# Latent attention's scores as three split fp32r products, with one PSUM copy moved from VectorE to ScalarE and the latents' squares added on GpSimd

## The chip, the cores and the metric

One core of a Trainium2 chip runs the whole program. The metric is the device time of one execution in microseconds (us). The kernel before was executed three times; what counts is the median. A further execution was profiled, and all rows below come from that one.

## The reference, cut to what matters

The program is two transformer blocks on 256 tokens (plus 16 meta tokens in the first), with a model width of 1024: a state-space mixer, an MLP, multi-head latent attention (MLA), an MLP, and then a block with neighbourhood attention, a short gated convolution and an MLP. The change lies nearly all in the latent attention:

```
q_lat, kv_lat, k_pe = split(h @ w_in, [384, 640])
q  = rms_norm(q_lat, q_a_g) @ w_q_b      # 16 heads x 96
kv = rms_norm(kv_lat, kv_a_g) @ w_kv_b   # 16 heads x (64 + 64)
k  = concat(k_nope, k_pe for all heads); v = the other 64
q, k = rms_norm(q, q_norm_g), rms_norm(k, k_norm_g)
q, k = the last 32 of each turned by the rotary angles
p  = softmax(q @ k.T * 96 ** -0.5, causal, two query blocks of 128)
o  = (p @ v) @ w_out
```

## The kernel before, in words

**Split products.** Every weight page (128 partitions x 1024 elements) is loaded by SP into `w_raw`, rounded by ScalarE (ACT) to fp32r (`w_hi`, helper `hi`), and VectorE (DVE) subtracts to get the rest (`w_lo`, helper `lo`). TensorE (PE) then forms hi*hi + hi*lo + lo*hi as three fp32r matmuls. Activations are split the same way. Other matmuls (scores, values, transposes) take plain fp32 operands; such a matmul appears as two records in the trace.

**The attention's steps.** PE, ACT and DVE each run their own hand-written loop over steps t = 0 to 21 (22 on ACT and DVE). GpSimd (POOL) follows them with a short list. Heads come in pairs i = 0 to 7. An even step t = 2i makes keys and values of pair i (`key_unit`), an odd step t = 2i + 1 its queries (`query_unit`). The work of a pair is spread over later steps:

- ACT squares the raw keys or queries (`unit_square`), DVE sums them (`unit_sum`, `k_ss` or `q_ss`), ACT takes logarithm and exponential (`unit_inv`, `k_inv` or `q_inv`), DVE scales in the next step (`unit_scaled`, `k_n` or `q_n`). Rotary turning of the queries is on DVE for the first three pairs (`turn_query`), on POOL afterwards (`query_rope`).
- PE transposes them (`turn_keys` in step 2i + 1, `turn_queries` at the end of step 2i + 2) into one PSUM area, `turned`, that keys and queries share.
- ACT scales that area into SBUF (`unit_final(t - 1)`: `k_fin` in step 2i + 1, `q_fin` in step 2i + 2). In every odd step but one this comes after `unit_inv(t)`, which itself waits for DVE's sum; step 15 has the two the other way round.
- PE makes the scores of head n in step n + 3 (`scores`), DVE masks them and takes the maximum in step n + 4 (`maxima`), ACT exponentiates (`exps`), DVE normalises in step n + 5 (`weigh`), PE transposes the probabilities in step n + 6 (`p_transposes`).
- The transposed probabilities go from PSUM to SBUF in two copies, 128x384 on DVE (`p_t_copy`) and 16x256 on ACT (`p_t0_copy`); PE multiplies them with the values once per pair (`values`), and ACT and DVE split the result (`o_high`, `o_low`).

The output projection (`mout_part`) is cut into parts that run among the last steps.

**Places that the prediction speaks of.** `scores` L740, `turn_keys` L713 with its wait for `qfin_done`, `turn_queries` L731 with its wait for `kfin_done`, PE's loop L804, `unit_final` L1266, `p_t0_copy` L1292, ACT's loop L1302, `unit_sum` L1770, `unit_scaled` L1816, `p_t_copy` L1850, DVE's loop L1860. Before the loop, PE sums squares of the latents over partitions with one-column fp32 matmuls: six matmuls at L658 for keys and values, six at L673 for queries (`q_stat`). At the program's start DVE makes the rest of the first small weight page (`lo(Page(0))`) after the last two `raw_lo`. In the second block's projections DVE makes `yb_lo` at the end of loop turns 11 and 12, and begins each of the turns 8 to 15 with the copy `p_t2` out of PSUM.

## Time and profile before

| | us |
|---|---|
| median of 3 runs | 1103.89 (1103.84 to 1104.99) |
| profiled execution, its own time | 1103.82 |
| span of the profile, first to last instruction | 1102.1 |
| PE busy | 1094.4 (99%) |
| DVE busy | 771.8 (70%) |
| ACT busy | 653.9 (59%) |
| POOL busy | 170.6 (15%) |

The span is 1.7 us shorter than the execution's time. The profile's times for one matmul overlap the next (about 280 ns of duration at about 120 ns from start to start), so costs on PE are read from start to start. A busy time of 99% on PE says that hardly anything else shows as a wait; DVE and ACT have slack on average, and the question is how that slack lies in the attention's steps, at 456 to 545 us of the span.

### The profile page before, as it was taken

The page shows a single profiled execution, that of the slowest core. Times are in us where ns is not written, and L with a number is a line of the kernel's source. Part 1 is how long each engine was busy: PE and PEld are TensorE (multiplying, and loading weights), DVE is VectorE, ACT ScalarE, POOL GpSimd, SP SyncE. Part 2 cuts the span into 40 slices and gives each one's busy share as a digit, 9 for nine tenths or more (in the row PEclk, how much of TensorE's full clock was granted, in tenths as well). Part 3 has the DMA queues.
Part 4 walks back from the last instruction along what each step waited for, and adds up shares of the span by engine and source line. Part 5 has one row for each costly group of instructions (what it writes and reads, how often), then busy time and mean ns, then how long its engine had stood idle before and what let it go on. Part 6 is the DMA issues. An engine that isn't in the chain of part 4 may idle for free.

```text
span 1102.1 us, 24005 instructions
## 1 busy us (share of the span) xinstructions
PE 1094.4 (99%) x8963; PEld 1066.9 (97%) x8963; DVE 771.8 (70%) x1153; ACT 653.9 (59%) x1075; POOL 170.6 (15%) x152
## 2 busy tenths in 40 slices
PE   9999999999999999999999999999999999999998
PEld 8999999999999999988899999999999999999998
DVE  8999999778665555688676665558787687666543
ACT  7899999555554343577565554446555755554331
POOL 0445444326000000111010000000003201000000
PEclk9999999999999999999999999999999999999999
DMA  7454444575454555332265555555444555555552
GB/s 267 181 186 163 169 157 173 153 249 172 171 171 172 179 178 175 136 135 98 83 218 177 189 189 181 180 193 173 153 154 154 185 181 190 180 182 191 187 180 90
DMA packets 53226, 189.96 MB, mean 172 GB/s; under 512 B 5920, under 2 KB 7200, under 8 KB 53168
## 3 DMA queue, kind: packets, MB, share of 16 engines
q1 hardware_dynamic: 51408, 182.59, 48.4%
q0 software_dynamic: 1760, 6.59, 2.1%
q8 instruction: 38, 0.62, 0.2%
q14 instruction: 20, 0.16, 0.0%
HBM read 188.07 MB, written 1.08 MB: 172 GB/s over the span
## 4 chain that ended last, share of the span: by engine, by line
PE 85%; DVE 10%; ACT 2%; issue 2%; DMA 1%; POOL 0%; SPq 0%; DVEq 0%; ACTq 0%
PE lin L462 27%; PE lin L464 26%; PE lin L463 26%; DVE w_lo L1430 3%; DMA w_raw<-w 1%; PE ps L561 1%; DVE s_m L1836 1%; DVE x_lo L1440 1%; DVE p_t L1854 1%; ACT w_hi L948 0%; ACT pr L1351 0%; DVE s_m L1918 0%; PE ps L540 0%; DVE p_t L1941 0%; DVE q_ss L1779 0%
## 5 line engine op out<-in xcount | busy, mean ns | idle before, releaser
L1430 DVE TENSOR_TENSOR w_lo<-w_raw,w_hi 128x1024 fp32r<-128x1024 f32 (+3 forms) x318 | 392.6, 1237 | 237.6 <-ACT w_hi L948 236.6
L948 ACT ACTIVATE w_hi<-w_raw 128x1024 fp32r<-128x1024 f32 (+2 forms) x342 | 352.0, 1034 | 230.9 <-PE lin L464 222.0
L462 PE MATMUL lin<-x_hi,w_hi 128*128 128x256 f32 (+1 forms) x1504 | 432.1, 287 | 0.4 <-DVE x_lo L1440 0.4
L464 PE MATMUL lin<-x_hi,w_lo 128*128 128x256 f32 (+1 forms) x1504 | 428.3, 285 | 0.0
L463 PE MATMUL lin<-x_lo,w_hi 128*128 128x256 f32 (+1 forms) x1504 | 427.3, 284 | 0.0
L462 PEld LDWEIGHTS lin<-x_hi,w_hi 128*128 128x128 f32 x1504 | 283.6, 189 | 2.2 <-issue 0.8
L464 PEld LDWEIGHTS lin<-x_hi,w_lo 128*128 128x128 f32 x1504 | 283.8, 189 | 0.0
L463 PEld LDWEIGHTS lin<-x_lo,w_hi 128*128 128x128 f32 x1504 | 283.0, 188 | 0.6
L464 PE MATMUL lin<-hid_hi,w_lo 128*128 128x256 f32 (+1 forms) x768 | 218.2, 284 | 0.0
L463 PE MATMUL lin<-hid_lo,w_hi 128*128 128x256 f32 (+1 forms) x768 | 217.9, 284 | 0.0
L462 PE MATMUL lin<-hid_hi,w_hi 128*128 128x256 f32 (+1 forms) x768 | 217.4, 283 | 0.0
L464 PEld LDWEIGHTS lin<-hid_hi,w_lo 128*128 128x128 f32 x768 | 145.1, 189 | 0.0
L462 PEld LDWEIGHTS lin<-hid_hi,w_hi 128*128 128x128 f32 x768 | 145.0, 189 | 0.0
L463 PEld LDWEIGHTS lin<-hid_lo,w_hi 128*128 128x128 f32 x768 | 144.3, 188 | 0.0
L2060 POOL TENSOR_TENSOR h_sq<-h_sq 128x256 f32<-128x256 f32 (+1 forms) x35 | 30.7, 878 | 448.1 <-ACT h_sq L961 446.6
L1171 ACT ACTIVATE relu<-lin 128x512 f32<-128x512 f32 (+1 forms) x48 | 29.1, 606 | 82.6 <-PE lin L464 82.6
L2065 POOL TENSOR_TENSOR w_lo<-w_raw,w_hi 128x1024 fp32r<-128x1024 f32 x24 | 58.4, 2437 | 70.2 <-ACT w_hi L948 70.0
L957 ACT ACTIVATE x_hi<-h,vecs 128x256 fp32r<-128x256 f32 (+2 forms) x40 | 20.3, 507 | 41.6 <-DVE h L1708 37.7
L462 PE MATMUL lin<-g_hi,w_hi 128*128 128x272 f32 x144 | 42.3, 294 | 0.1
L1691 DVE TENSOR_TENSOR hid_lo<-relu_sq,hid_hi 128x512 f32 (+1 forms) x48 | 34.4, 717 | 11.2 <-DVE relu_sq L1687 11.2
L464 PE MATMUL lin<-g_hi,w_lo 128*128 128x272 f32 x144 | 41.7, 289 | 0.0
L463 PE MATMUL lin<-g_lo,w_hi 128*128 128x272 f32 x144 | 41.4, 288 | 0.0
(301 smaller groups left out, 1505.5 us busy)
## 6 DMA issues: line engine op xcount, KB each, us to landing
w_raw<-w SPq DMA_DIRECT2D x342, 512.0 KB, 3.3
acs_bc<-acs_dram POOLq DMA_DIRECT2D x8, 544.0 KB, 5.9
bias_mask<-rpb POOLq DMA_DIRECT2D x4, 512.0 KB, 10.9
h<-h SPq DMA_DIRECT2D x4, 272.0 KB, 3.7
out<-h SPq DMA_DIRECT2D x8, 128.0 KB, 3.3
cst<-const SPq DMA_DIRECT2D x1, 808.0 KB, 7.1
vecs<-vec SPq DMA_DIRECT2D x1, 131.5 KB, 2.1
w_raw<-w SPq DMA_DIRECT2D x1, 128.0 KB, 4.7
```

Of the source, the lines that this page charges most:

```text
L462: mm3(o, wh, xh, start=first and i == 0, stop=False)
L463: mm3(o, wh, xl, start=False, stop=False)
L464: ins = mm3(o, wl, xh, start=False, stop=last and i == kts - 1)
L561: nc.tensor.matmul(o[rows, 0:T], x_tok[:, 0, j * HD:(j + 1) * HD], mm[:, j, 0:T], start=True, stop=False)
L948: a(w_hi[pg.slot][:, 0:n], w_raw[pg.slot][:, 0:n], ACT.Copy).then_inc(w_hi_done, pages)
L957: a(x_hi[:, kt.value, 0:width(norm)], h[:, kt.value, tokens(norm)], ACT.Copy, scale=gain(norm, kt.value)).then_inc(xh_done, 1)
L1171: a(relu[i][:, :, 0:n], linp(k, slice(0, n)), ACT.Relu).then_inc(drained[k.parity], 1)
L1430: tt(w_lo[pg.slot][:, 0:n], w_raw[pg.slot][:, 0:n], w_hi[pg.slot][:, 0:n].bitcast(F32), ALU.subtract)\
L1440: stt(x_lo[:, kt.value, 0:n], h[:, kt.value, tk], gain(norm, kt.value), x_hi[:, kt.value, 0:n].bitcast(F32), ALU.mult, ALU.subtract).then_ ...
L1691: tt(hid_lo[:, bass.ds(at.value, 2), 0:n], relu_sq[i][:, :, 0:n], hid_hi[:, bass.ds(at.value, 2), 0:n].bitcast(F32), ALU.subtract).then_in ...
L2060: tt(h_sq[:, 0, 0:n], h_sq[:, 0, 0:n], h_sq[:, kt, 0:n], ALU.add).then_inc(hsum_done, 1)
L2065: tt(w_lo[pg.slot][:, 0:n], w_raw[pg.slot][:, 0:n], w_hi[pg.slot][:, 0:n].bitcast(F32), ALU.subtract)\
```

## The change

Scores: queries and keys are kept as fp32r pairs (`q_hi`, `q_lo`, `k_hi`, `k_lo`) and each of a head's two products becomes three. ACT's `unit_final` writes the rounded part; a new `unit_low` on DVE subtracts it from the same PSUM area, and only DVE's write now sets `kfin_done` and `qfin_done`. The 128x384 copy of the probabilities goes to ACT, ahead of the 16x256 copy. POOL adds neighbouring squares of latents, so that PE sums three columns in place of six at the first place and four in place of six at the second. Parts of the output projection, the split of the first page and `yb_lo` are put elsewhere in their engines' order.

```diff
-        q_fin = [sb(f"q_fin{i}", [QK, 4, T2], F32, mla) for i in range(2)]
-        k_fin = [sb(f"k_fin{i}", [QK, 4, T], F32, mla) for i in range(2)]
+        q_hi = [sb(f"q_hi{i}", [QK, 4, T2], F32R, mla) for i in range(2)]
+        q_lo = [sb(f"q_lo{i}", [QK, 4, T2], F32R, mla) for i in range(2)]
+        k_hi = [sb(f"k_hi{i}", [QK, 4, T], F32R, mla) for i in range(2)]
+        k_lo = [sb(f"k_lo{i}", [QK, 4, T], F32R, mla) for i in range(2)]
...
-            pe.wait_ge(latsq_done, 1)
+            pe.wait_ge(latsum_done, 1)
             for b, t0 in enumerate(MLA_BLOCKS):
-                for i in range(2):
-                    ins = nc.tensor.matmul(ps5[:, b:b + 1], lat_sq[:, i, t0:t0 + P], ones[:, 0:1],
-                                           start=i == 0, stop=i == 1)
+                ins = nc.tensor.matmul(ps5[:, b:b + 1], lat_sq[:, 0, t0:t0 + P], ones[:, 0:1], start=True, stop=True)
...
-                pe.wait_ge(latsq_done, 3)
+                pe.wait_ge(latsum_done, 2)
...
-                    for i in range(3):
+                    for i in range(2):
...
-                nc.tensor.matmul(o[:, 0:144], q_fin[p][:, j, 0:128], k_fin[p][:, j, 0:144], start=True, stop=True)
-                nc.tensor.matmul(o[:, 144:416], q_fin[p][:, j, 128:256], k_fin[p][:, j, :],
-                                 start=True, stop=True).then_inc(s_done, 1)
+                for to, queries, keys in ((slice(0, 144), slice(0, 128), slice(0, 144)),
+                                          (slice(144, 416), slice(128, 256), slice(0, T))):
+                    for i, (q_, k_) in enumerate(((q_hi, k_hi), (q_hi, k_lo), (q_lo, k_hi))):
+                        ins = mm3(o[:, to], q_[p][:, j, queries], k_[p][:, j, keys], start=i == 0, stop=i == 2)
+                ins.then_inc(s_done, 1)
...
-                if t == 17:
-                    mout_part(0, 5, 0)
...
                 if 3 <= t < 19:
                     scores(t - 3)
+                if t == 16:
+                    mout_part(0, 4, 0)
...
-                    mout_part(0, 2, 5)
+                    mout_part(0, 3, 4)
...
-                    a(q_fin[s % 2][:, hs, :], turned, ACT.Copy, scale=v(V_QG, rows=slice(0, QK))).then_inc(qfin_done, 1)
+                    a(q_hi[s % 2][:, hs, :], turned, ACT.Copy, scale=v(V_QG, rows=slice(0, QK))).then_inc(qhi_done, 1)
...
+                a(p_t[n % 2][:, :], ps7[:, 0:384], ACT.Copy).then_inc(pt_done, 1)
                 a(p_t0[n % 2][0:META, :], ps4[0:META, 256:512], ACT.Copy).then_inc(pt0_done, 1)
...
+            lo(Page(0), DT_PAGE)
+            dve.sem_inc(w_lo_done[1], 1)
             raw_lo(6)
             raw_lo(7)
-            lo(Page(0), DT_PAGE)
-            dve.sem_inc(w_lo_done[1], 1)
...
+            def unit_low(un):
+
+                i, s = un // 2, un // 4
+                j0 = 2 * (i % 2)
+                hs = slice(j0, j0 + 2)
+                if s >= 2:
+                    dve.wait_ge(s_done, 4 * (s - 2) + j0 + 2)
+                if un % 2:
+                    dve.wait_ge(qhi_done, i + 1)
+                    stt(q_lo[s % 2][:, hs, :], turned, v(V_QG, rows=slice(0, QK)),
+                        q_hi[s % 2][:, hs, :].bitcast(F32), ALU.mult, ALU.subtract).then_inc(qfin_done, 1)
+                else:
+                    dve.wait_ge(khi_done, i + 1)
+                    stt(k_lo[s % 2][:, hs, META:T], turned, v(V_KG, rows=slice(0, QK)),
+                        k_hi[s % 2][:, hs, META:T].bitcast(F32), ALU.mult, ALU.subtract)
+                    stt(k_lo[s % 2][:, hs, 0:META], turned_meta, v(V_KG, rows=slice(0, QK)),
+                        k_hi[s % 2][:, hs, 0:META].bitcast(F32), ALU.mult, ALU.subtract).then_inc(kfin_done, 1)
...
-                if t == 15:
-                    p_t_copy(t - 6)
...
-                if 6 <= t < 15 and t % 2:
-                    p_t_copy(t - 6)
...
-                if 6 <= t < 16 and not t % 2 or 16 <= t < MLA_STEPS:
-                    p_t_copy(t - 6)
+                if 1 <= t <= 16:
+                    unit_low(t - 1)
...
+            add_latents(0, 1)
             pool.wait_ge(kpe_step, 2)
...
+            add_latents(4, 3)
             pool.wait_ge(kpefin_done, 3)
```

`yb_lo` moves from the end of turns 11 and 12 to turns 12 and 13, right after the copy `p_t2`. `add_latents(to, count)` waits for `count` of the squares and adds two 128x272 tiles on POOL.

DVE's order at the end of an odd step, here t = 7 (sum of the queries' squares) and the start of the next. Before:

```order
L1430 TENSOR_TENSOR w_lo<-w_raw,w_hi 128x576 [waits w_hi_done]
L1854 COPY p_t<-ps 128x384 [waits pT_done]
L1779 TENSOR_REDUCE q_ss<-q_sq 128x4 [waits qln_done,qsq_done]
L1823 TENSOR_TENSOR q_n<-lin,q_inv 128x384 [waits qT_done,qinv_done]
L1858 TENSOR_TENSOR o_lo<-ps,o_hi 128x256 [waits oh_done]
```

With the change:

```order
L1435 TENSOR_TENSOR w_lo<-w_raw,w_hi 128x576 [waits w_hi_done]
L1784 TENSOR_REDUCE q_ss<-q_sq 128x4 [waits qln_done,qsq_done]
L1868 SCALAR_TENSOR_TENSOR k_lo<-lin,vecs,k_hi 96x2x256 [waits khi_done]
L1870 SCALAR_TENSOR_TENSOR k_lo<-ps,vecs,k_hi 96x2x16
L1828 TENSOR_TENSOR q_n<-lin,q_inv 128x384 [waits qT_done,qinv_done]
L1875 TENSOR_TENSOR o_lo<-ps,o_hi 128x256 [waits oh_done]
```

The copy has left, and between the sum and the scaling of the queries stand two subtractions that wait for ACT's `k_hi`.

ACT's order in the same odd step, with the change (squares of the queries to the rounding of the keys):

```order
L1245 ACTIVATE q_sq<-lin 128x4x96 [waits qss_done,w_used]
L1300 ACTIVATE p_t<-ps 128x384 [waits pT_done]
L1301 ACTIVATE p_t<-ps 16x256
L1292 ACTIVATE pr,rsum<-s_m,nmx 128x144 [waits pT_done,sm_done]
L1292 ACTIVATE pr,rsum<-s_m,nmx 128x272
L1256 ACTIVATE q_ln<-q_ss 128x4 [waits qss_done]
L1260 ACTIVATE q_inv<-q_ln,eps_t 128x4 [waits qn_done,qln_done]
L1282 ACTIVATE k_hi<-lin,vecs 96x2x256 [waits kT_done]
L1283 ACTIVATE k_hi<-ps,vecs 96x2x16
```

The order is that of before but for the 128x384 copy, which is new here; `k_hi` has the place that `k_fin` had, behind `q_ln` and `q_inv`.

DVE's order at the end of an even step (sum of the keys' squares), before, in t = 6:

```order
L1787 TENSOR_REDUCE k_ss<-k_sq 128x6 [waits kln_done,ksq_done]
L1798 TENSOR_TENSOR v_tok<-lin,kv_inv 128x384 [waits w_used]
L1854 COPY p_t<-ps 128x384 [waits pT_done]
L1830 TENSOR_TENSOR k_n<-lin,k_inv 128x6x64 [waits kT_done,kinv_done]
```

With the change:

```order
L1792 TENSOR_REDUCE k_ss<-k_sq 128x6 [waits kln_done,ksq_done]
L1803 TENSOR_TENSOR v_tok<-lin,kv_inv 128x384 [waits w_used]
L1864 SCALAR_TENSOR_TENSOR q_lo<-lin,vecs,q_hi 96x512 [waits qhi_done]
L1835 TENSOR_TENSOR k_n<-lin,k_inv 128x6x64 [waits kT_done,kinv_done]
```

`q_lo` takes the place of the copy, with a wait for ACT's `q_hi`.

## Rows read from the trace of the kernel before

**Rows 1.** The page: the granted clock of TensorE over 40 slices, in tenths.
```profile
PEclk9999999999999999999999999999999999999999
```

**Rows 2.** Timeline of PE, steps 12 and 13: start us, duration us, line, tiles, records.
```profile
503.93 0.39 PE L682 MATMUL lin<-w_hi,l_hi 128*128 128x256 f32 x1
...
506.15 0.41 PE L754 MATMUL ps<-k_fin,q_fin 96*128 96x144 f32 x2
...
506.86 0.27 PE L768 MATMUL ps<-cst,pr 128*16 128x128 f32 x1
...
513.24 0.38 PE L682 MATMUL lin<-w_hi,l_hi 128*128 128x256 f32 x1
```

**Rows 3.** Timeline of DVE, end of step 12 to the start of step 14.
```profile
507.15 0.55 DVE L1787 TENSOR_REDUCE k_ss<-k_sq 128x6 f32<-128x390 f32 x1
...
508.09 0.54 DVE L1854 COPY p_t<-ps 128x384 f32<-128x384 f32 x1
508.55 0.54 DVE L1830 TENSOR_TENSOR k_n<-lin,k_inv 128x384 f32<-128x384 f32 x1
...
511.41 0.55 DVE L1779 TENSOR_REDUCE q_ss<-q_sq 128x4 f32<-128x388 f32 x1
512.56 0.56 DVE L1823 TENSOR_TENSOR q_n<-lin,q_inv 128x384 f32<-128x384 f32 x1 [0.60 <-ACT q_inv L1256]
```

**Rows 4.** Timeline of ACT, the same steps.
```profile
508.11 0.68 ACT L1275 ACTIVATE q_fin<-lin,vecs 96x512 f32<-96x512 f32 x1
...
511.99 0.21 ACT L1252 ACTIVATE q_ln<-q_ss 128x4 f32<-128x4 f32 x1
...
513.00 0.27 ACT L1279 ACTIVATE k_fin<-ps,vecs 96x32 f32<-96x32 f32 x1
```

**Rows 5.** Timeline of DVE: first and last of eight key scalings, last query scaling.
```profile
460.39 0.56 DVE L1830 TENSOR_TENSOR k_n<-lin,k_inv 128x384 f32<-128x384 f32 x1 [0.43 <-ACT k_inv L1264]
...
518.65 0.55 DVE L1830 TENSOR_TENSOR k_n<-lin,k_inv 128x384 f32<-128x384 f32 x1
...
523.13 0.56 DVE L1823 TENSOR_TENSOR q_n<-lin,q_inv 128x384 f32<-128x384 f32 x1 [0.60 <-ACT q_inv L1256]
```

**Rows 6.** DVE's waits, 458 to 522 us: total us, times, longest.
```profile
DVE o_lo L1858 <- ACT o_hi L1300: 4.3, 4, 1.4
...
DVE w_lo L1430 <- ACT w_hi L948: 0.6, 1, 0.6
```

**Rows 7.** Timeline of DVE in the second block: two three-operand instructions in a row.
```profile
756.88 0.88 DVE L1983 SCALAR_TENSOR_TENSOR qk_f<-qk_r,vecs,qk_inv 128x256 f32<-128x256 f32 x2
```

**Rows 8.** Timeline of PE, steps 16 and 17: waits, last query transposes, values.
```profile
524.17 0.27 PE L768 MATMUL ps<-cst,pr 128*16 128x128 f32 x1 [0.39 <-DVE o_lo L1858]
...
525.37 0.64 PE L737 MATMUL lin<-cst,q_n 128*96 128x128 f32 x4 [0.50 <-POOL q_n L2160]
...
529.07 0.65 PE L784 MATMUL ps<-p_t,v_tok 128*64 128x256 f32 x4
```

**Rows 9.** Timeline of DVE and of ACT, steps 16 and 17.
```profile
525.86 1.21 DVE L1430 TENSOR_TENSOR w_lo<-w_raw,w_hi 128x1024 fp32r<-128x1024 f32 x1
526.99 0.29 DVE L1836 CUSTOM_DVE_ANT_0 s_m<-ps,cst 128x144 f32<-128x144 f32 x1
...
527.58 0.15 DVE L1844 RECIPROCAL rinv<-rsum 128x2 f32<-128x2 f32 x1
...
527.69 0.41 ACT L1288 ACTIVATE pr<-s_m,nmx 128x144 f32<-128x144 f32 x1
...
528.61 0.36 ACT L1296 ACTIVATE p_t<-ps 16x256 f32<-16x256 f32 x1
```

**Rows 10.** Timeline of PE at the three smaller places.
```profile
10.40 0.31 PE L505 MATMUL lin<-g_hi,w_hi 128*32 128x272 f32 x1 [0.33 <-DVE w_lo L1430]
...
448.18 1.39 PE L658 MATMUL ps<-cst,h_sq 128*128 128x1 f32 x12
...
833.79 1.08 PE L902 MATMUL ps<-p_t,v 128*64 128x256 f32 x8 [0.66 <-DVE p_t L1941]
```

More of the change, by code:

```diff
@@ L1274, in unit_final @@
                     act.wait_ge(qT_done, i + 1)
-                    a(q_fin[s % 2][:, hs, :], turned, ACT.Copy, scale=v(V_QG, rows=slice(0, QK))).then_inc(qfin_done, 1)
+                    a(q_hi[s % 2][:, hs, :], turned, ACT.Copy, scale=v(V_QG, rows=slice(0, QK))).then_inc(qhi_done, 1)
                 else:
                     act.wait_ge(kT_done, i + 1)
-                    a(k_fin[s % 2][:, hs, META:T], turned, ACT.Copy, scale=v(V_KG, rows=slice(0, QK)))
-                    a(k_fin[s % 2][:, hs, 0:META], turned_meta, ACT.Copy, scale=v(V_KG, rows=slice(0, QK)))\
-                        .then_inc(kfin_done, 1)
+                    a(k_hi[s % 2][:, hs, META:T], turned, ACT.Copy, scale=v(V_KG, rows=slice(0, QK)))
+                    a(k_hi[s % 2][:, hs, 0:META], turned_meta, ACT.Copy, scale=v(V_KG, rows=slice(0, QK)))\
+                        .then_inc(khi_done, 1)
             def exps(n):
@@ L1941, in _ @@
                     nc.vector.tensor_copy(p_t2[i % 2][:, :], ps7[:, :]).then_inc(pt2_done, 1)
+                if i in (12, 13):
+                    j = i - 12
+                    dve.wait_ge(ybh_done, j + 1)
+                    tt(yb_lo[:, 2 * j:2 * j + 2, :], yb[:, 2 * j:2 * j + 2, :],
+                       yb_hi[:, 2 * j:2 * j + 2, :].bitcast(F32), ALU.subtract).then_inc(ybl_done, 1)
                 if i in (11, 12):
@@ L2132, in _, with add_latents @@
                     .then_inc(rope_done, 1)
+            def add_latents(to, count):
+                pool.wait_ge(latsq_done, count)
+                tt(lat_sq[:, to, :], lat_sq[:, to, :], lat_sq[:, to + 1, :], ALU.add).then_inc(latsum_done, 1)
+            add_latents(0, 1)
             pool.wait_ge(kpe_step, 2)
```

17 lines of the change are left out of this document (4 added, 13 removed).

## The prediction, made before the change ran

> **What bounds the kernel now.** I read the page first: TensorE is busy 99% of the span, and its granted clock is full in every slice [rows 1]. Then I read PE's timeline through the attention. Steps 12 and 13 make one pair of heads and take 513.24 - 503.93 = 9.31 us [rows 2], with every product starting right behind the one before: there PE sets the pace. Next come the timelines of DVE and ACT over the same pair, because the change hangs new work on both. They show an order of hand-overs that is nearly as long as PE's work. From one `k_n` to the next there are DVE's instructions, 0.60 us of idleness before `q_n` [rows 3], and a wait of up to 1.4 us for `o_hi` before `o_lo`, four times and 4.3 us in all [rows 6]. The first is a hand-over to ACT and back and cannot shrink. The second is the only slack in the loop; from 508.55 us DVE runs without a gap to the end of `q_ss`. So DVE has about 1 us per pair to give before it sets the pace in place of PE. The question is how much the change puts on it, as work and as waiting.
>
> **Scores on PE.** In step 12 the two fp32 products of a head take 506.86 - 506.15 = 0.71 us from their start to the next work [rows 2]. Afterwards there are six fp32r products at 0.11 to 0.12 us each, 0.69 us. That is 0.02 us a head in the even steps; in odd steps the product's entry behind a transpose of 16 rows is slower now, and 0.2 us could come back. Over 16 heads that is 0.3 to 1.9 us of PE work saved, but worth nothing where PE is made to wait.
>
> **DVE in the odd steps.** Before, `q_ss` starts at 511.41 and `q_n` at 512.56: 1.15 us [rows 3]. In the new order `k_lo` stands between the two and waits for ACT's `k_hi`, which ACT makes only after `q_ln` and `q_inv`, and these wait for `q_ss`. So DVE waits for an ACT chain that it has just set going. From the start of `q_ss` to `q_ln` it is 511.99 - 511.41 = 0.58 us; from there to the end of the last `k_fin`, 513.00 + 0.27 = 513.27, it is 1.28 us [rows 4]; a hand-over costs 0.03 us (`q_inv` to `q_n`). Then the two subtractions. No row shows this form with 512 elements out of PSUM. Two of 256 elements end 0.88 us after the first starts [rows 7], which fits 0.40 us from start to start, or 0.13 us plus 1.04 ns an element: 0.66 us for 512, 0.17 us for 32, both estimates. The bounds are 0.60 (a two-operand instruction's pace) and 0.88 us. Together 0.58 + 1.28 + 0.03 + 0.83 = 2.72 us in place of 1.15: **+1.57 us** in each of the seven odd steps 1 to 13, so +11.0 us. The removed copy, 508.55 - 508.09 = 0.46 us [rows 3], gives back 4 x 0.46 = 1.8 us (steps 7, 9, 11, 13).
>
> The Trainium skill, in "VectorE: DVE Perf Modes", section "The DRAIN you can't avoid", says that a next instruction does not start until the pipe has emptied, save one that is not held. The rows here show starts 0.08 us before the predecessor's end; by the page's rule taken strictly each new subtraction would cost its full duration, about 0.25 us more a pair, and the sum would come out 2 us higher.
>
> **DVE in the even steps.** Before, `k_ss` at 507.15 and the next `k_n` at 508.55: 1.40 us, with the copy in it [rows 3]. Now `q_lo` waits for `q_hi`, whose forerunner ends at 508.11 + 0.68 = 508.79 [rows 4]: 1.64 + 0.03 + 0.66 = 2.33 us, **+0.93 us** in steps 6, 8, 10, 12, 14, and +1.39 us in steps 2 and 4, which had no copy: +7.4 us.
>
> **The loop as a whole.** From the first `k_n` at 460.39 to the eighth at 518.65 it is 58.3 us [rows 5]. Added to DVE's chain are 11.0 - 1.8 + 7.4 = 16.6 us; the waits for `o_hi` (4.3 us) and one for `w_hi` (0.6 us) vanish [rows 6], because those partners are then early. Net **+11.7 us**: 70.0 us for seven pairs. A late pair takes 10.1 us against PE's 9.3, so PE now waits in each, before `turn_keys` (for `q_lo`) or `turn_queries` (for the `q_n` that stands behind `k_lo`). ACT gains two copies of 0.5 us a pair, ahead of waits that it has anyway; their cover is the gap between `q_sq` and `q_ln`. If it is gone, each costs up to 0.5 us, some 2 us in all.
>
> **The end of the loop.** In step 15 ACT makes `k_hi` before `q_inv`; from `k_n` to `q_n`, 4.48 us before [rows 5], goes to about 4.2: -0.3 us. The first part of the projection, 12 products and 1.4 us, now stands in step 16, where PE waits 0.39 and 0.50 us [rows 8]. It covers these waits, but it also stands behind the last `k_lo` and ahead of the last `turn_queries`, which comes about 0.4 us later after `q_n`. From `turn_queries` to `values(5)` it was 529.07 - 525.37 = 3.70 us [rows 8]. The new chain is 0.1, ACT's two copies 0.75, `q_hi` 0.68, `q_lo` 0.69, then on DVE a full `w_lo` 1.13 and `maxima` 0.59, ACT's `exps` 0.92 and only behind them the two copies again, 0.75: 5.7 us [rows 9]. That is +2.0, with the above **+2.4 us**. Lower bound 0 (if later slack takes it), upper 3.5. Three products moved behind the last values add 0.36 and take away a wait of 0.2: +0.2.
>
> **The small parts.** First page earlier: PE waits 0.33 us for it [rows 10]; -0.3 us, nothing behind is late for want of the two `raw_lo`. Squares: the first place loses 6 of 12 records in 1.39 us, -0.65 us; POOL is free from 446 us and its sum, 0.8 us, ends before PE asks at 448.2. The second place saves 0.4 us on PE, but `k_n` does not depend on it: 0. If POOL were late, PE would wait at most 1 us at either. `yb_lo` behind `p_t2` brings that copy 0.6 us forward, against a wait of 0.66 us on PE [rows 10]: -0.6 us, as nothing late waits for `yb_lo` itself.
>
> **Sum:** 11.7 - 0.3 + 2.4 + 0.2 - 0.3 - 0.65 - 0.6 = +12.4 us. On the profiled execution's 1103.8 us, which is the median within 0.1 us, that is **1116.2 us**.
>
> **Rivals.**
> 1. *PE keeps the pace, the change is faster.* This is so if DVE's new waits lie beside its slack. It needs an added chain of under 1 us a pair, where I count over 2; it decides at the `q_ss`, `k_hi`, `k_lo`, `q_n` sequence. For it speaks PE's 99% and DVE's 70%. Then the gains are 0.3 + 0.65 + 0.4 + 0.6 + 0.9 in step 16, and 0.3 to 1.9 for the scores: about -4, **1100 us**. Chance 0.09.
> 2. *Only the first pairs stretch.* They have less PE work, and DVE already sets their pace: three pairs cost 3 x 1.57 + 2 x 1.39 + 0.93 - 0.6 = +7.8 us; the later four (chain +2.0 each, slack 1.1) may be absorbed if the hand-overs are shorter than mine. With the small gains and without the end's term +6: **1110 us**. Chance 0.15.
> 3. *The clock falls.* PE would stand idle for 1 to 2 us in each pair. The rows show the full 2.4 GHz with idle pieces of 0.5 us only [rows 1, 8]. If half the loop ran at 1.2 GHz, some 35 us of PE work would take as long again: **1150 us**. The Trainium skill ("TensorE: Matmul & The Clock Gate", "HAM oscillation") describes a kernel whose waits between groups of matmuls brought the clock down each time. Chance 0.04.
> 4. *The change gives no more than noise*, its terms cancelling: chance 0.02.
>
> My forecast has 0.70; within it the bounds (0.60 to 0.88 us for a subtraction, 0 to 3.5 at the end, up to 2 for ACT) give 1112 to 1120. The range is 1107 to 1120: it takes in rival 2 and leaves out 1 and 3. A measurement here tells 0.2%, 2.2 us, from no change. Faster 0.09, same 0.03, slower 0.88.
>
> **What would show it.** In the profile after: `k_n` to `k_n` near 10 us in late pairs; DVE idle before `k_lo` about 1.3 us, released by ACT `k_hi`, and about 0.7 us before `q_lo`, released by `q_hi`; no more waits before `o_lo` in the loop; PE idle before the transposes, released by `q_lo` and by POOL's or DVE's `q_n`. I am wrong if pairs stay at 9.3 us with PE gapless, if the DVE subtractions take under 0.5 us, or if the span grows outside 440 to 560 us.

## The result, and the profile after

| | before | after |
|---|---|---|
| median, us | 1104.15 (1103.84 to 1104.99) | 1123.08 (1120.64 to 1124.25) |
| ratio | | 1.0168, 95% interval 1.0156 to 1.0181 |
| profiled execution, its own time | 1103.82 | 1122.26 |
| span | 1102.1 | 1120.6 |

Each median is of four executions. The change made the kernel slower by 1.7%. The direction was forecast, the size was not: 1116.2 us were forecast, with a range that ended at 1120.

The span falls into four stretches by three marks on DVE: the first `k_n`, the eighth `k_n` and the last `o_lo` (the start of each). Every profile below is read by them.

| us | to the first `k_n` | seven pairs | close (to the last `o_lo`) | rest |
|---|---|---|---|---|
| before | 460.4 | 58.3 | 25.2 | 558.3 |
| forecast | 459.4 | 70.0 | 27.5 | 557.7 |
| after | 460.0 | 70.6 | 32.0 | 558.0 |

So the loop came out as forecast within 0.6 us, and 4.5 of the profiled execution's 6.1 us above the forecast lie in the close. The page of after, against [rows 1]:

```profile
span 1120.6 us, 24067 instructions
...
PE 1102.3 (98%) x8985; PEld 1074.6 (96%) x8985; DVE 776.8 (69%) x1161; ACT 659.7 (59%) x1091; POOL 172.1 (15%) x154
...
PEclk9999999999999999989899999999999999999999
```

Two slices no longer have the full clock. DVE's timeline answers to [rows 3, 5]: one even step, one odd step, and the first and last `k_n`.

```profile
460.00 0.56 DVE L1835 TENSOR_TENSOR k_n<-lin,k_inv 128x384 f32<-128x384 f32 x1 [0.43 <-ACT k_inv L1268]
...
506.85 0.55 DVE L1792 TENSOR_REDUCE k_ss<-k_sq 128x6 f32<-128x390 f32 x1
508.55 0.75 DVE L1864 SCALAR_TENSOR_TENSOR q_lo<-lin,vecs,q_hi 96x512 fp32r<-96x512 f32 x1 [0.69 <-ACT q_hi L1279]
509.22 0.54 DVE L1835 TENSOR_TENSOR k_n<-lin,k_inv 128x384 f32<-128x384 f32 x1
...
511.60 0.55 DVE L1784 TENSOR_REDUCE q_ss<-q_sq 128x4 f32<-128x388 f32 x1
513.57 0.75 DVE L1868 SCALAR_TENSOR_TENSOR k_lo<-lin,vecs,k_hi 96x512 fp32r<-96x512 f32 x1 [1.42 <-ACT k_hi L1283]
514.24 0.24 DVE L1870 SCALAR_TENSOR_TENSOR k_lo<-ps,vecs,k_hi 96x32 fp32r<-96x32 f32 x1
514.40 0.54 DVE L1828 TENSOR_TENSOR q_n<-lin,q_inv 128x384 f32<-128x384 f32 x1
...
530.57 0.54 DVE L1835 TENSOR_TENSOR k_n<-lin,k_inv 128x384 f32<-128x384 f32 x1
```

From `q_ss` to `q_n` it is 2.80 us (forecast 2.72), from `k_ss` to `k_n` 2.37 (forecast 2.33). A subtraction of 512 elements takes 0.67 us from start to start (forecast 0.66). The next instruction again starts 0.08 us ahead of the recorded end, so the stricter reading of the Trainium skill ("VectorE: DVE Perf Modes", "The DRAIN you can't avoid") does not hold here either. The table of waits, 458 to 562 us (total, times, longest), against [rows 6]:

```profile
DVE k_lo L1868 <- ACT k_hi L1283: 9.8, 8, 1.4
DVE o_lo L1875 <- ACT o_hi L1305: 7.4, 3, 3.4
DVE q_lo L1864 <- ACT q_hi L1279: 7.2, 8, 2.4
PEld lin L728 <- DVE k_n L1835: 6.1, 6, 2.1
...
PE ps L788 <- ACT p_t L1300: 2.4, 1, 2.4
...
PE ps L772 <- ACT p_t L1301: 1.9, 5, 0.7
```

DVE stands still 17 us for the high halves. The last two lines are waits of PE that the forecast does not name: PE waits for ACT's copies of the probabilities. PE's timeline at the close, against [rows 8]:

```profile
533.73 1.12 PE L788 MATMUL ps<-p_t,v_tok 128*64 128x256 f32 x4
...
539.05 0.60 PE L739 MATMUL lin<-cst,q_n 128*96 128x128 f32 x4
540.14 0.27 PE L772 MATMUL ps<-cst,h_sq 128*16 128x128 f32 x1 [0.49 <-ACT p_t L1301]
544.91 1.12 PE L788 MATMUL ps<-p_t,v_tok 128*64 128x256 f32 x4 [2.45 <-ACT p_t L1300]
```

The last queries' transposes (L739) start 8.48 us after the eighth `k_n`, where it was 6.72, and `values(5)` 5.86 us after them, where it was 3.70. The four products of L788 take 1.12 us twice, 0.65 in [rows 8]. The windows of after (length; busy us of PE, PE's weight loads, DVE, ACT and POOL; granted clock, share of DMA, GB/s) show one candidate for the reason:

```profile
462.00:482.00 20.00, 15.29 (x114) 13.94 (x113) 14.46 (x40) 12.28 (x35) 1.02 (x2) 0.91 0.36 121
482.00:500.00 18.00, 17.26 (x134) 15.72 (x133) 14.74 (x49) 12.11 (x39) 2.50 (x6) 0.91 0.29 101
500.00:520.00 20.00, 18.95 (x159) 16.71 (x160) 15.63 (x45) 14.40 (x48) 3.98 (x10) 1.00 0.32 102
520.00:540.00 20.00, 17.80 (x135) 14.50 (x132) 14.78 (x46) 14.68 (x45) 3.45 (x9) 0.91 0.25 84
540.00:560.00 20.00, 16.37 (x116) 14.16 (x117) 8.28 (x29) 8.80 (x26) 0.00 (x0) 0.83 0.17 54
```

With only the levels 2.4 and 1.2 GHz, a mean of 0.91 over 20 us is 3.6 us at the lower one; the four windows below 1.00 make 3.6 + 3.2 + 3.6 + 6.8 = 17 us. The trace places them: the granted clock is 0.50 from 478.5 to 485.3 us in the pairs, and from 533.1 to 536.5 and from 543.4 to 550.2 us in the close. The profiled execution is no exception: over whole executions the mean granted clock was 0.992 to 0.995 in all four of the changed kernel and 0.999 or 1.000 in those of the kernel before. In DVE's timeline of the close the order costs time as well:

```profile
540.66 0.75 DVE L1864 SCALAR_TENSOR_TENSOR q_lo<-lin,vecs,q_hi 96x512 fp32r<-96x512 f32 x1 [2.35 <-ACT q_hi L1279]
541.33 1.21 DVE L1435 TENSOR_TENSOR w_lo<-w_raw,w_hi 128x1024 fp32r<-128x1024 f32 x1
542.46 0.30 DVE L1841 CUSTOM_DVE_ANT_0 s_m<-ps,cst 128x144 f32<-128x144 f32 x1
```

The maxima of head 13, whose scores PE had made by 537.1, wait behind `q_lo` and a weight page. Last, the scores themselves, one head in an even step: 505.15 to 505.86, 0.71 us as in [rows 2]. Six fp32r products take as long as two fp32 products, so PE gains nothing.

```profile
505.15 0.23 PE L759 MATMUL ps<-k_hi,q_hi 96*128 96x144 f32 x1
...
505.86 0.27 PE L772 MATMUL ps<-cst,pr 128*16 128x128 f32 x1
```

### The profile page after: what moved, and what is told of

Same layout as the page of the kernel before. It is cut to its first block, busy times and chain, and to the rows that moved or that the text cites. A ratio compares the mean times of both kernels' runs of the same rounds, so it can differ in the third digit from the quotient of the medians.

```text
span 1120.6 us, 24067 instructions
## 1 busy us (share of the span) xinstructions
PE 1102.3 (98%) x8985; PEld 1074.6 (96%) x8985; DVE 776.8 (69%) x1161; ACT 659.7 (59%) x1091; POOL 172.1 (15%) x154
## 4 chain that ended last, share of the span: by engine, by line
PE 85%; DVE 7%; ACT 2%; issue 2%; DMA 1%; POOL 0%; DVEq 0%; ACTq 0%; SPq 0%
PE lin L466 26%; PE lin L468 26%; PE lin L467 26%; DVE w_lo L1435 2%; DMA w_raw<-w 1%; PE ps L565 1%; DVE s_m L1841 1%; DVE x_lo L1445 1%; ACT q_hi L1279 0%; PE ps L759 0%; PE ps L895 0%; DVE k_n L1835 0%; PE ps L906 0%; PE ps L544 0%; PE ps L881 0%
## 5 line engine op out<-in xcount | busy, mean ns | idle before, releaser
L1696 DVE TENSOR_TENSOR hid_lo<-relu_sq,hid_hi 128x512 f32 (+1 forms) x48 | 34.4, 717 | 11.2 <-DVE relu_sq L1692 11.2
```

The source lines that it names most:

```text
L1696: tt(hid_lo[:, bass.ds(at.value, 2), 0:n], relu_sq[i][:, :, 0:n], hid_hi[:, bass.ds(at.value, 2), 0:n].bitcast(F32), ALU.subtract).then_in ...
```

## The experiments

The four stretches of each profile, the median of the timed executions, and its ratio to the kernel before (1103.9 to 1104.5 us in these runs). The median and the profile are in general different executions. Of hi_first one execution of four took 5774 us, for which nothing on record gives a reason; its median is that of the other three.

| run | first `k_n` | pairs | close | rest | median | ratio (95%) |
|---|---|---|---|---|---|---|
| late_low | 459.9 | 61.6 | 29.4 | 558.1 | 1113.1 | 1.0078 (1.0064 to 1.0092) |
| hi_first | 459.4 | 64.8 | 30.0 | 558.1 | 1117.9 | 1.0124 (1.0106 to 1.0143) |
| late_hi | 460.1 | 63.1 | 29.5 | 558.0 | 1114.1 | 1.0096 (1.0083 to 1.0110) |
| copy_dve | 460.6 | 72.4 | 29.6 | 558.0 | 1123.9 | 1.0184 (1.0170 to 1.0198) |
| late_copy_dve | 461.7 | 64.2 | 31.7 | 558.0 | 1117.2 | 1.0106 (1.0088 to 1.0124) |
| copy_act | 460.7 | 58.2 | 26.4 | 558.3 | 1105.3 | 1.0008 (0.9999 to 1.0017) |
| more_products | 461.9 | 71.1 | 30.0 | 558.0 | 1121.4 | 1.0146 (1.0130 to 1.0161) |
| mout_back | 459.6 | 70.0 | 27.3 | 558.0 | 1119.9 | 1.0151 (1.0132 to 1.0170) |
| close_order | 462.7 | 70.6 | 26.7 | 558.1 | 1119.3 | 1.0135 (1.0115 to 1.0155) |
| late_best | 462.1 | 61.6 | 27.3 | 558.1 | 1110.6 | 1.0051 (1.0036 to 1.0067) |
| small_parts | 459.4 | 58.1 | 25.9 | 558.1 | 1104.7 | 1.0006 (0.9997 to 1.0015) |
| small_lat_yb | 459.6 | 58.1 | 25.2 | 558.1 | 1102.9 | 0.9991 (0.9982 to 1.0000) |
| first_page | 463.1 | 58.3 | 25.2 | 558.4 | 1105.9 | 1.0009 (1.0000 to 1.0018) |
| page_back | 459.4 | 70.1 | 30.9 | 558.0 | 1120.0 | 1.0145 (1.0129 to 1.0160) |

### The loop: order or amount of work

**late_low**, DVE's loop:

```diff
                 if 1 <= t <= 16:
                     unit_scaled(t - 1)
+                if 2 <= t <= 17:
+                    unit_low(t - 2)
...
-                if 1 <= t <= 16:
-                    unit_low(t - 1)
```

> The changed kernel, but DVE writes the low half of a unit's keys or queries one step later, right behind the scaling of the next unit, instead of last in its own step, where it waits for ACT's high half (waits of 1.2 us in the mean for k_hi, 0.9 for q_hi, and all of them stand in the chain). Theory A, the order: the 10.1 to 10.4 us of a pair come from DVE standing still for ACT's high half while the next unit waits behind it. Then a pair falls by about 1.2 us in the odd steps and the whole loop by 6 to 9 us: 1114 to 1117 us, between the two kernels, with the waits of k_lo and q_lo on ACT gone from the table of waits. Theory B, the amount of work on DVE and ACT sets the pair (each low half costs DVE 0.7 to 0.9 us that the kernel before did not have): the waits move to another place and the time stays at 1121 to 1125 us. Against A from the other side: the transposes of the next keys need the low half of the queries read out of the shared bank first, so the low half stands ahead of the transposes now, and 0.6 us of the gain can be lost there.

The order decides: 10 us less in the median with the same instructions, a little more than theory A said. The profile is 11.5 us shorter, 8.9 of them in the pairs. Nothing stands between sum and scaling any more, 1.07 and 1.20 us, and `q_lo` comes with no wait behind `k_n` (DVE's timeline):

```profile
510.30 0.55 DVE L1792 TENSOR_REDUCE k_ss<-k_sq 128x6 f32<-128x390 f32 x1
...
511.37 0.56 DVE L1835 TENSOR_TENSOR k_n<-lin,k_inv 128x384 f32<-128x384 f32 x1
512.02 0.75 DVE L1864 SCALAR_TENSOR_TENSOR q_lo<-lin,vecs,q_hi 96x512 fp32r<-96x512 f32 x1
...
514.61 0.55 DVE L1784 TENSOR_REDUCE q_ss<-q_sq 128x4 f32<-128x388 f32 x1
515.81 0.56 DVE L1828 TENSOR_TENSOR q_n<-lin,q_inv 128x384 f32<-128x384 f32 x1 [0.66 <-ACT q_inv L1260]
```

The granted clock was 1.00 in every window of this profile. The close, 29.4 us, is therefore not to be set against the 32.0 us of after as they stand: further down, 3.5 of those turn out to be the clock, so in the close the later low halves cost about 0.9 us (the last queries' transposes start 9.4 us after the eighth `k_n`, where at full clock it is 7.3). What is left in the pairs, 3.4 us above before, is what the order does not remove. 2.8 of it lie in the first three pairs (6.6, 7.5 and 9.5 us against 5.9, 6.6 and 8.2), the ones of which rival 2 says that DVE sets their pace; that it is DVE's amount of work was argued, not tested.

**hi_first**, ACT's loop: `unit_final(t - 1)` ahead of `unit_inv(t)` in every odd step, not in step 15 alone.

```diff
-                if t == 15:
+                if 1 <= t < 16 and t % 2:
                     unit_final(t - 1)
                 if t < 16:
                     unit_inv(t)
```

> The changed kernel, but in the odd steps ACT writes the keys' high half before the logarithm and the exponential of the queries' norm, instead of behind them. Theory A, the hand-over between ACT and DVE (q_ss, then k_hi, then k_lo, then q_n, 2.72 us where the kernel before took 1.15) sets the odd step: k_lo then runs while ACT makes the queries' norm, and 0.6 to 0.8 us of each odd step goes away, 4 to 5.5 us in all, 1117.5 to 1119 us. Theory B, the amount of work: nothing is removed, so 1122 to 1124 us. A third outcome, the high half comes before the transposes are there and ACT stands still with the norm behind it: a slower kernel, 1124 us or more.

As theory A expected, 1117.9 us. From `q_ss` to `q_n` it is 1.95 us here, 0.85 less than in after; over the seven odd steps it is 6.2 us less, against 5.8 us which the pairs lost. The profiled execution, 1113.9 us, is the fastest of the three by 4 us. DVE's timeline:

```profile
516.28 0.55 DVE L1784 TENSOR_REDUCE q_ss<-q_sq 128x4 f32<-128x388 f32 x1
517.40 0.75 DVE L1868 SCALAR_TENSOR_TENSOR k_lo<-lin,vecs,k_hi 96x512 fp32r<-96x512 f32 x1 [0.57 <-ACT k_hi L1283]
...
518.23 0.55 DVE L1828 TENSOR_TENSOR q_n<-lin,q_inv 128x384 f32<-128x384 f32 x1
```

**late_hi** has both edits, the two diffs above together.

> Both orders together: DVE's low halves one step later, and ACT's high half of the keys ahead of the queries' norm in the odd steps. Alone they gave 10 us and 5 us. If both remove the same wait (DVE's low half of the keys standing still for ACT's high half, 9.8 us in eight waits), the second adds nothing, or costs up to 5 us, since the queries' scaling now waits 0.7 us longer for the norm in every odd step: 1113 to 1118 us. If they remove different waits, the sum shows: 1108 to 1110 us.

The second edit adds nothing to the first and costs 1.5 us in the pairs: both remove the same wait, and `q_n` now waits 8.3 us for `q_inv`, where it was 5.1 in late_low.

### The copy of the probabilities

**copy_act** is the kernel before with the copy on ACT:

```diff
             def p_t0_copy(n):
...
+                a(p_t[n % 2][:, :], ps7[:, 0:384], ACT.Copy).then_inc(pt_done, 1)
...
-                if 6 <= t < 15 and t % 2:
-                    p_t_copy(t - 6)
```

(and so for the other two calls of `p_t_copy` in DVE's loop). **copy_dve** is the changed kernel with the same lines the other way round.

> The changed kernel with the probabilities' 128x384 copy back on DVE in the places of the kernel before, everything else as changed. By the prediction's term the copy is worth 1.8 us on DVE, so this is slower than the changed kernel by about that: 1125 us. Rival, from the trace of the changed kernel: with both copies on ACT the transposes of the next head wait for them (1.9 us in five waits) and the values too (2.4 us in one), mostly behind the last pair, and the close of the stage took 32.0 us from the last scaled keys to the last low half of the outputs, where it was 25.1 us before; with the copy on DVE that close shrinks by 2 to 4 us and the loop grows by up to 2 us, 1120 to 1123 us.

> The kernel before with one part of the change alone: the probabilities' 128x384 copy on ACT. Prediction's term: 1.8 us less on DVE in the pairs' even steps, 1102.4 us. Rival: DVE's place in the pair's chain was hidden or ACT is as full as DVE, 1104 us. Second rival: the close of the stage waits for ACT, which makes each copy behind a weight page's high half or two exponentials, +1 to +4 us, 1105 to 1108 us.

In the changed kernel the pairs grow by 1.8 us with the copy back on DVE, the prediction's term to the tenth, and the close shrinks by 2.4; the medians cannot tell the two kernels apart. Most of the 2.4 us is not the copy: the close of after has 10.2 us at a granted clock of 0.50, that of copy_dve 3.4 us. hi_first, whose instructions in the close stand in the order of after and which also has 3.4 us at 0.50 there, closes in 30.0 us, so about 0.4 us are left for the copy. In the kernel before, the copy on ACT changes nothing in the pairs (58.2 and 58.3 us) and loses 1.3 us at the close: 0.7 ahead of the last queries' transposes, 0.4 from there to `values(5)`, where PE waits for it, and 0.2 behind (PE's timeline of copy_act; no wait before `values(5)` in [rows 8]):

```profile
526.35 0.64 PE L737 MATMUL lin<-cst,q_n 128*96 128x128 f32 x4 [0.50 <-POOL q_n L2149]
530.42 0.65 PE L784 MATMUL ps<-p_t,v_tok 128*64 128x256 f32 x4 [0.41 <-ACT p_t L1296]
```

**late_copy_dve** is late_low with the lines of copy_dve.

> The kernel with the low halves one step later (1113.1 us), and the probabilities' copy back on DVE. In that kernel DVE is the fuller engine of the loop (15.9 to 17.8 us of 20), so by its load 8 copies of about 0.4 us in the even steps cost up to 3 us in the loop. At the close the values wait 1.3 us and the outputs' high half for ACT's copies. If the close decides, 1110 to 1112 us; if the loop decides, 1114 to 1116 us.

The pairs grow by 2.6 us, as DVE's load said. The close did not shrink but grew by 2.2, which neither case foresaw. The growth lies in the two stretches in which the clock was down, from the eighth `k_n` to the last queries' transposes (9.4 to 10.4 us) and from `values(5)` to `values(7)` (13.5 to 14.8 us); between them it is 4.7 us in both. The windows, where late_low had 1.00:

```profile
520.00:540.00 20.00, 16.18 (x122) 13.99 (x118) 16.19 (x48) 12.72 (x34) 3.48 (x9) 0.91 0.25 79
540.00:560.00 20.00, 18.71 (x145) 16.03 (x144) 9.28 (x30) 6.67 (x23) 0.00 (x0) 0.91 0.15 50
```

### The close, and the clock

**more_products** (the diff shows the first of its three places) repeats a unit's first product five times ahead of `query_unit(i >= 1)` and `key_unit(1 to 3)`, one product of `scores(14)` eight times and the last transpose of `p_transposes(11)` eleven times; the results of the repeats are overwritten.

```diff
+                    for _ in range(again if i == 0 else 0):
+                        mm3(o, lh, wh, start=True, stop=True)
                     mm3(o, lh, wh, start=i == 0, stop=False)
```

> The changed kernel with products repeated on TensorE (their first result thrown away) in the places of the loop where PE stood still before the granted clock fell: ahead of the queries' products of each pair, of the keys' products of pairs 1 to 3, of the scores of head 14 and of the last transposes of head 11. It only adds work to PE. Theory C, the granted clock: the changed kernel lost some 3 to 4 us against the forecast to three stretches at 1.2 GHz (17 us in all, of which PE works the smaller part on the path), so with the clock kept at 2.4 GHz it takes 1118 to 1121 us although it does more. Theory D, the excess comes from waits alone: the added products cost 0 to 5 us, 1123 to 1128 us, whatever the clock does. If the clock falls all the same, the run tells nothing between the two.

With more work on PE the median is 1.7 us below the changed kernel's, and the clock stayed at 1.00 up to 540 us (0.91 after it). The time lies between the two cases, nearer to C. The single executions say more: in three of the four the granted clock was 1.00 over the whole execution, and they took 1118.6, 1121.0 and 1121.7 us, where after took 1120.6 to 1124.3 at 0.992 to 0.995. The fourth, the profiled one with 1122.7 us, also has the long `sg` that is described under the small parts. So work added in the places where PE had stood still kept the clock up: PE's standing still is what brings it down here. What that costs, the next two runs show.

**mout_back**, PE's loop:

```diff
+                if t == 17:
+                    mout_part(0, 5, 0)
...
-                if t == 16:
-                    mout_part(0, 4, 0)
...
-                    mout_part(0, 3, 4)
+                    mout_part(0, 2, 5)
```

> The changed kernel with the output's products in the order of the kernel before: none ahead of the last queries' transposes, 15 behind them, 6 instead of 9 ahead of the last values. The prediction took this part of the change at +0.2 us. The kernel with the small parts alone closes the stage 0.8 us later than the kernel before, although its loop is the same. Theory A: the 12 products (1.4 us) stand ahead of the last queries' transposes and hold the whole close up by about 1 us, and the 3 products ahead of the last values by 0.35 us, so undoing them gives 1.0 to 1.4 us: 1121.8 us. Theory B: in the changed kernel PE stands still there for other engines anyway, so the time stays at 1123 us within 0.4, or grows, because the products that filled PE are gone and the granted clock falls more.

**close_order**, DVE's loop: `maxima(13)` and `weigh(12)` ahead of the last `q_lo`.

```diff
-                if 1 <= t <= 16:
+                if 1 <= t < 16:
                     unit_low(t - 1)
-                if t in (16, 17):
-                    lo(At(C_HEAD).page(nxt))
+                if t == 17:
+                    unit_low(15)
+                    lo(At(C_HEAD).page(18))
+                    lo(At(C_HEAD).page(19))
```

> The changed kernel with one step of DVE in another order: the maxima and the weighing of the scores' heads 13 and 12 come ahead of the last low half of the queries, which waited 2.35 us for ACT's high half with them behind it, and the two weight pages' low halves follow it. Theory A, a wait that holds the engine's queue: this gives 1.5 to 2.5 us at the close of the stage (32.0 us from the last scaled keys to the last low half of the outputs in the changed kernel), 1120.5 to 1121.5 us. Theory B, the granted clock made the close long: the close stays at 31 to 32 us and the clock falls in it as before, 1122.5 to 1124 us.

Both medians gained more than either case said, 3.2 and 3.8 us. In close_order PE has the same instructions in the same order as in after, and its windows have the full clock at the close (windows, then PE's timeline):

```profile
520.00:540.00 20.00, 17.62 (x147) 15.13 (x145) 16.90 (x50) 15.81 (x46) 4.00 (x10) 1.00 0.33 106
540.00:560.00 20.00, 17.77 (x149) 15.27 (x148) 8.36 (x30) 10.07 (x31) 0.00 (x0) 1.00 0.15 54
```

```profile
536.26 0.65 PE L788 MATMUL ps<-p_t,v_tok 128*64 128x256 f32 x4
...
540.65 0.60 PE L739 MATMUL lin<-cst,q_n 128*96 128x128 f32 x4
...
544.75 0.65 PE L788 MATMUL ps<-p_t,v_tok 128*64 128x256 f32 x4 [0.68 <-ACT p_t L1300]
...
558.25 0.65 PE L788 MATMUL ps<-p_t,v_tok 128*64 128x256 f32 x4
```

So the two profiles price the clock. From the eighth `k_n` to L739: 540.65 - 533.34 = 7.3 us, 8.5 in after. From `values(5)` to `values(7)`: 558.25 - 544.75 = 13.5 us, 15.9 in after (544.91 to 560.78). Together 3.5 us of after's close are TensorE at 1.2 GHz. Between the two, from L739 to `values(5)`, 4.1 us stand against 5.9: that is the order on DVE, 1.8 us. Page_back (below), in which PE, DVE and ACT have after's order in the close, tells the two apart, because its clock was down in one of the stretches only (windows of page_back):

```profile
520.00:540.00 20.00, 17.22 (x142) 14.61 (x140) 15.45 (x42) 15.11 (x43) 3.50 (x9) 1.00 0.25 80
540.00:560.00 20.00, 17.16 (x125) 14.56 (x125) 6.71 (x28) 7.30 (x25) 0.00 (x0) 0.83 0.16 53
```

The close in five profiles, us, with the mean granted clock of each stretch:

| profile | eighth `k_n` to L739 | L739 to `values(5)` | `values(5)` to `values(7)` |
|---|---|---|---|
| after | 8.5 (0.80) | 5.9 (0.87) | 15.9 (0.83) |
| page_back | 7.3 (1.00) | 5.9 (0.87) | 15.9 (0.83) |
| close_order | 7.3 (1.00) | 4.1 (1.00) | 13.5 (1.00) |
| mout_back | 6.6 (1.00) | 5.8 (1.00) | 13.1 (1.00) |
| before (L737) | 6.7 (1.00) | 3.7 (1.00) | 13.0 (1.00) |

The same instructions in the same order take 1.2 us longer in the first stretch when the clock is down for 3.4 us of it. Mout_back had the full clock from 500 us on as well, and its close, 27.3 us, is 1.2 below the 32.0 - 3.5 = 28.5 of after without its slow stretches: that is the 12 products ahead of the last queries' transposes (0.7) and the three ahead of the last values (0.4). In the pairs the clock cost less: with 6.8 us at 1.2 GHz after and close_order took 70.6 us, with 3.4 us page_back and mout_back took 70.1 and 70.0, and the whole difference is in the third pair (11.2 and 11.3 against 10.7 us).

The clock fell in different places from one execution to the next, also of one kernel. Its mean was 0.997, 0.993, 0.997 and 0.997 in close_order, and in mout_back the time followed it: 1116.7 and 1119.4 us at 0.998, 1119.9 and 1121.3 at 0.995, 1124.0 at 0.992. The profile of mout_back is the fastest of its five executions, so its parts price the edits and its total does not stand for the median.

**late_best** joins late_low, mout_back, and the last `q_lo` behind the weighing (the lines of close_order; the diff is against late_low):

```diff
-                if 2 <= t <= 17:
+                if 2 <= t < 17:
                     unit_low(t - 2)
```

> Low halves one step later on DVE (1113.1 us, close 29.4 us), with the output's products in the order of the kernel before and the last low half of the queries behind the maxima and the weighing. If the waits found in the close are what is left of it: close 26 to 27.5 us, the whole 1110 to 1111.5 us. The loop keeps its 61.7 us against 58.3 us of the kernel before, which is DVE's added work of 0.75 us in every odd step, so no order of this form gets to the kernel before; a time under 1106 us would speak against that.

As expected in the close and in the median, and the granted clock was 1.00 in all five executions. It is the best form of the split that was tried, and still 0.5% behind the kernel before.

### The small parts

**small_parts** is the kernel before with every small part of the change; **small_lat_yb** has the latents' squares and `yb_lo` alone.

```diff
+            def add_latents(to, count):
+                pool.wait_ge(latsq_done, count)
+                tt(lat_sq[:, to, :], lat_sq[:, to, :], lat_sq[:, to + 1, :], ALU.add).then_inc(latsum_done, 1)
```

> The kernel before, with all the small parts of the change and without the split of the scores and without the probabilities' copy on ACT: latents' squares added on GpSimd, the first page's halves in another order, the low half of the inner products moved, the three products of the output moved. By the sum of the prediction: -0.65 (squares), -0.6 (low half of the inner products), -0.3 (first page), +0.2 (three products), so 1.3 us under the kernel before, a ratio of 0.9988. By the trace of the changed kernel, where the first page's 0.39 us are given back by two waits of 0.2 us before 441 us: 1.0 to 1.1 us under, a ratio of 0.9990. If the small parts disturb one another, 0 or slower.

> The kernel before with two of the small parts alone, the latents' squares added on GpSimd (0.65 us by the prediction) and the low half of the inner products moved (0.6 us); the order of the output's products and the first page are those of the kernel before. If the two keep what the trace shows of them, 1.25 us under the kernel before, 1102.9 us, ratio 0.9989, and the kernel beats both. The kernel with all the small parts was level with the kernel before (1.0006), where its moved output products gave back 0.8 us at the close and its first page at most 0.4; so 0.5 us under is the least that this explains. If it is level as well, the gains of these parts are taken by something that no part of the trace names, the arrival of the weight pages first.

Level with all four, 1.1 us gained with two, as expected; with an interval that ends at 1.0000 the gain is at the edge of what can be told here. The output's products give 0.8 us back at the close. By the profile the two parts of small_lat_yb gained unequally. The first `k_n` comes 0.75 us earlier, with the six records at L658 in 0.72 us in place of 1.39. But `yb_lo` gained 0.3 us and not 0.6: the third set of value products at L902 starts 0.6 us earlier after the last `o_lo`, as forecast, the fourth only 0.3, and so it is in every profile with this edit (the rest is 558.0 to 558.1 us against 558.3). What is missing between small_parts and small_lat_yb beyond the 0.8 us was put down to the first page, and tested.

**first_page** is the kernel before with that edit alone, **page_back** the changed kernel without it.

```diff
-            raw_lo(6)
-            raw_lo(7)
             lo(Page(0), DT_PAGE)
             dve.sem_inc(w_lo_done[1], 1)
+            raw_lo(6)
+            raw_lo(7)
```

> The kernel before with one edit: the low half of the first page ahead of the last two residual low halves on DVE. Prediction: -0.3 us, 1103.9 us. Theory E: the edit shifts DVE against GpSimd by a few tenths of a microsecond, and in some executions one DVE instruction near 32 us is then held 2.5 us beside a GpSimd subtraction, which costs some 2 us on PE. Then the single times fall into two groups 2 to 2.5 us apart, a spread that the kernel before does not have (1103.4 to 1105.1 in nearly all executions), and the median is 0.3 to 1.5 us above the kernel before. If the spread stays within 1.5 us and the median within 0.3 us of the kernel before, the first page is not the cause.

> The changed kernel with the first page in the order of the kernel before. Theory E: its 1123.1 us fall by 0.5 to 1.5 us, 1121.6 to 1122.6 us, and the first scaled keys start within 0.5 us of 460 us in the profile. Theory F, the spread comes from the split of the scores and the close alone (the granted clock falls in other places from execution to execution): 1123 us with the same spread of 3.6 us.

The single times of first_page fall into two groups, five at 1103.9 to 1104.8 and six at 1105.9 to 1107.2, as theory E said; the ratio, 1.0009, has an interval that begins at 1.0000. The profiled execution is of the second. Timelines of DVE, POOL and PE in it:

```profile
32.45 3.59 DVE L1543 TENSOR_SCALAR sg<-cv 128x544 f32<-128x544 f32 x2
36.59 1.21 DVE L1430 TENSOR_TENSOR w_lo<-w_raw,w_hi 128x1024 fp32r<-128x1024 f32 x1
...
33.29 2.43 POOL L2065 TENSOR_TENSOR w_lo<-w_raw,w_hi 128x1024 fp32r<-128x1024 f32 x1
...
39.71 0.73 PE L540 MATMUL ps<-bc_s 128*128 128x272 f32 x2 [0.99 <-DVE bc_s L1547]
```

The same in the kernel before:

```profile
31.86 1.10 DVE L1543 TENSOR_SCALAR sg<-cv 128x544 f32<-128x544 f32 x2
33.51 2.94 DVE L1430 TENSOR_TENSOR w_lo<-w_raw,w_hi 128x1024 fp32r<-128x1024 f32 x1
...
32.97 2.40 POOL L2065 TENSOR_TENSOR w_lo<-w_raw,w_hi 128x1024 fp32r<-128x1024 f32 x1 [0.27 <-ACT w_hi L948]
```

In both a DVE instruction takes longer than it does elsewhere, by 2.5 us here and by 1.7 us in the kernel before, and ends only after POOL's subtraction has ended (33.29 + 2.43 = 35.72 and 32.97 + 2.40 = 35.37 us). In the kernel before it is `w_lo`, which has time; in this execution it is the second `sg`, with everything to `bc_s` behind it, and PE waits 2.3 us for `bc_s` in two waits, the first of which the last line shows. `sg` starts 0.84 us ahead of POOL's subtraction here and 1.11 in the kernel before. That distance alone does not decide it: small_lat_yb has 0.86 in its profile and was not caught, though one of its eleven executions took 1105.95 us and the others at most 1103.64. Of the twelve profiles with the new first page, after's among them, five show the long `sg` (late_copy_dve, more_products, close_order, late_best, first_page); of the four without, none; after's does not. Page_back's median is 3.1 us below after's, more than the 0.5 to 1.5 expected, and the first page is not all of it. Its profile is 2.2 us shorter than after's, and neither has the long `sg`: 0.6 us lie ahead of the first `k_n`, 0.5 in the pairs and 1.1 in the close, and the last two are the clock. What the edit is worth in the changed kernel's median was not separated from that.

## Why the prediction was wrong

- **DVE in the odd and in the even steps, the loop as a whole**: right, step by step. 2.80 us against 2.72, 2.37 against 2.33, 0.67 against 0.66 for the subtraction, 70.6 against 70.0 for seven pairs. The copy's -1.8 us was measured as 1.8. Two small errors are hidden in the sum: in steps 2 and 4 the growth was 1.24 us and not 1.39 (1.07 us before), and about 0.5 of the 70.6 us is TensorE at 1.2 GHz, which the sum did not hold.
- **The end of the loop** is the step that failed: "+2.4 us", bounds 0 to 3.5. With the 0.2 for three products and the -0.3 of step 15, 2.3 were summed and 6.9 measured (25.2 to 32.0 us). Its chain from `turn_queries` to `values(5)` was nearly right, 5.9 us against 5.7 (the terms as written add up to 5.6). What was missing: PE at 1.2 GHz, 3.5 us, and the 12 products ahead of `turn_queries`. The latter were taken to cover waits and to cost 0.1 with what step 15 gives; at full clock `turn_queries` came 0.6 us later, and mout_back puts both moved pieces at 1.2 us, where 0.4 and 0.2 were summed. Of the 4.5 us by which the close exceeded the forecast, the clock is 3.5.
- **Rival 3, the clock falls**, was right in its mechanism and was kept out of the sum. It was priced as half the loop at 1.2 GHz, 1150 us, with a chance of 0.04; 17 us at 1.2 GHz came, and cost 3.5 us at the close and about 0.5 in the pairs. It is shown that PE's standing still brought the clock down: with work put in its place (more_products) three executions of four kept it at 1.00, none of the changed kernel did. The Trainium skill, in the section that the prediction names ("TensorE: Matmul & The Clock Gate", "HAM oscillation"), has a kernel in which every wait between groups of matmuls brings the clock down; here PE waited in every pair, and the profile has three falls.
- **The small parts**: the squares' -0.65 came: 0.67 us at L658 itself. `yb_lo`'s -0.6 came as 0.3: the wait that it removes is gone, but half of the gain is taken back one set of products later. **First page**, -0.3 us with "nothing behind is late", did not come: the median of that edit alone is 1.5 us above the kernel before, with a ratio whose interval (1.0000 to 1.0018) leaves room for no change and none for a gain. What it left out is that the edit shifts DVE against POOL, and that in some executions `sg` is then held for 2.5 us and PE waits 2.3 us for `bc_s`.
- **Copies on ACT**: "ahead of waits that it has anyway" held in the loop and failed at the close, where the copies cost 1.3 us in the kernel before and about 0.4 in the changed one. Another 2.0 us between the closes of after and copy_dve are the clock.
- **Scores on PE**: nothing saved in the even steps (0.02 us a head forecast) and nothing in the odd ones.

The profiled execution adds up: 0.6 (pairs), 4.5 (close), 0.6 (ahead of the attention) and 0.3 (rest) make the 6.1 us above the forecast, within rounding. The median is 0.8 us above the profiled execution. The four executions lie 3.6 us apart, and the clock and the first page both vary between executions; which of them makes the 0.8 us was not seen. How near the total came is in part luck: the clock stays down for longer in one execution than in the next.

## What to carry to other kernels

When a step is split between two engines that already hand a chain to and fro, put the second half where its partner's result is already there: one line moved by one step was worth 10 us here, and no engine's load changed (by the profiles, about 4 of 11.5 us are TensorE's clock, which then stayed up). Price an edge of a loop with the clock that PE will have there, not with the one that it had, and give the clock a term in the sum as soon as PE is made to wait in every step. An edit that frees a few tenths on one engine can shift its instructions against another engine's and hold one of them up, so look at the spread of single executions and not at the median alone.
